# Seven key and value units of the memory between the stick-breaking heads

## What is computed

```python
# hgrn2 heads (4 of width 128) and stick-breaking heads (8 of width 64), side by side
z = jnp.einsum('bhtd,bhsd->bhts', q_blk, kh) * scale
log_beta = jax.nn.log_sigmoid(z)
log_one_minus = jnp.where(before, jax.nn.log_sigmoid(-z), 0.0)
between = lax.cumsum(log_one_minus, axis=3, reverse=True) - log_one_minus
weights = jnp.exp(jnp.where(before, log_beta + between, -jnp.inf))
o_sb = head_rmsnorm(weights @ v, sb_gnorm)
x = x + jnp.concatenate([o_hg, o_sb]) @ w_out
# cross-attention to a memory of 256 tokens, 4 heads of width 256
q = rmsnorm(x, mem_q_norm) @ w_q
k, v = jnp.split(rmsnorm(mem, mem_kv_norm) @ w_kv, 2)
x = x + (softmax(q @ k.T * 256 ** -0.5) @ v) @ w_o
```

## Time and profile before

| | us |
|---|---|
| median of 3 runs (lowest, highest) | 2531.74 (2530.05, 2534.24) |
| the profiled execution | 2530.41 |
| its span, first to last instruction | 2528.6 |
| PE busy in the span | 2443.9 (97%) |
| last step of Hgrn to the first values of Stick | 1821.9 to 1851.2 |
| values of head 0 to values of head 6 | 1851.2 to 1912.9 |
| values of head 6 to the end of the first unit of mix_out | 1912.9 to 1949.8 |
| key and value units | 1985.9 to 2028.0 |

### The profile page before, as it was taken

The page is one execution under the profiler, slowest core; times in us unless marked ns, Lnnn a source line. Parts: engine busy times, 40 slices in busy tenths (PEclk is TensorE's granted clock), DMA queues, the critical chain, the costliest instruction groups (busy, mean ns, idle before and its releaser), DMA issues.

```text
span 2528.6 us, 30307 instructions
## 1 busy us (share of the span) xinstructions
PE 2443.9 (97%) x12278; PEld 2034.2 (80%) x12278; DVE 1246.6 (49%) x1493; ACT 896.1 (35%) x1207; POOL 70.6 (3%) x80
## 2 busy tenths in 40 slices
PE   7989999999999999999999999999888999999998
PEld 6657888888899788888788888799866987888886
DVE  6687533357736543332444431546585645444423
ACT  3353333313344343331333321344444444333311
POOL 0210000000012000000000000000000000000000
PEclk9999999998999999999999999999988999999999
DMA  8125522363323122222222222221100322222221
GB/s 347 59 86 215 194 104 100 150 258 125 104 96 97 67 83 100 100 100 100 79 94 93 100 100 100 94 86 67 68 17 17 119 98 73 93 100 91 91 101 66
DMA packets 40408, 267.36 MB, mean 106 GB/s; under 512 B 4379, under 2 KB 5659, under 8 KB 9219
## 3 DMA queue, kind: packets, MB, share of 16 engines
q1 hardware_dynamic: 31248, 219.87, 24.2%
q0 software_dynamic: 5696, 40.37, 4.2%
q10 hardware_dynamic: 3378, 5.91, 0.8%
HBM read 263.90 MB, written 2.24 MB: 105 GB/s over the span
## 4 chain that ended last, share of the span: by engine, by line
PE 87%; DVE 7%; ACT 4%; issue 1%; DMA 0%; DVEq 0%; SPq 0%; ACTq 0%
PE bank L225 25%; PE bank L226 25%; PE bank L227 25%; DVE w_lo L212 1%; ACT w_hi L208 1%; PE bank L2107 1%; PE bank L328 1%; PE bank L2190 1%; PE bank L2202 1%; PE bank L1827 1%; DVE work L452 1%; PE bank L256 1%; DVE work L436 1%; PE bank L257 1%; PE bank L262 1%
## 5 line engine op out<-in xcount | busy, mean ns | idle before, releaser
L225 PE MATMUL bank<-h_hi,w_hi 128*128 128x512 f32 x1832 | 724.2, 395 | 5.4 <-DVE w_lo L212 2.2
L226 PE MATMUL bank<-h_lo,w_hi 128*128 128x512 f32 x1832 | 716.4, 391 | 0.0
L227 PE MATMUL bank<-h_hi,w_lo 128*128 128x512 f32 x1832 | 716.4, 391 | 0.0
L212 DVE TENSOR_TENSOR w_lo<-raw,w_hi 128x2048 fp32r<-128x2048 f32 x192 | 440.0, 2291 | 501.9 <-ACT w_hi L208 501.9
L208 ACT ACTIVATE w_hi<-raw 128x2048 fp32r<-128x2048 f32 x192 | 366.3, 1908 | 430.8 <-PE bank L227 425.6
L225 PEld LDWEIGHTS bank<-h_hi,w_hi 128*128 128x128 f32 x1832 | 346.0, 189 | 84.0 <-issue 6.7
L227 PEld LDWEIGHTS bank<-h_hi,w_lo 128*128 128x128 f32 x1832 | 345.8, 189 | 73.1
L226 PEld LDWEIGHTS bank<-h_lo,w_hi 128*128 128x128 f32 x1832 | 346.0, 189 | 71.8 <-issue 1.4
L227 PE MATMUL bank<-g_hi,w_lo 128*128 (+1 forms) x704 | 273.9, 389 | 0.0
L225 PE MATMUL bank<-g_hi,w_hi 128*128 (+1 forms) x704 | 273.9, 389 | 0.0
L226 PE MATMUL bank<-g_lo,w_hi 128*128 (+1 forms) x704 | 273.9, 389 | 0.0
(11 more groups left out here) (298 smaller groups left out, 2760.7 us busy)
## 6 DMA issues: line engine op xcount, KB each, us to landing
raw<-stream SPq DMA_DIRECT2D x192, 1024.0 KB, 4.8
work<-stream POOLq DMA_DIRECT2D x19, 1024.0 KB, 7.0
h_plain<-stream POOLq DMA_DIRECT2D x16, 1024.0 KB, 5.4
work<-stream SPq DMA_DIRECT2D x13, 1024.0 KB, 12.3
work<-mlstm_rows ACTq DMA_DIRECT2D x8, 512.0 KB, 5.0
x<-xT SPq DMA_DIRECT2D x1, 2048.0 KB, 9.6
outT<-work SPq DMA_DIRECT2D x8, 256.0 KB, 2.2
work<-mlstm_rows ACTq DMA_DIRECT2D x8, 192.0 KB
```

What stands on the lines that cost most here:

```text
L212: nc.vector.tensor_tensor(w_lo[:, slot(m), :], raw[:, slot(m), :], w_hi[:, slot(m), :], ALU.subtract).then_inc(lo_split, 1)
L225: nc.tensor.matmul(out, stationary[0], moving[0], start=first, stop=False)
L226: nc.tensor.matmul(out, stationary[0], moving[1], start=False, stop=False)
L227: return nc.tensor.matmul(out, stationary[1], moving[0], start=False, stop=last)
```

## The change

- `PLAN`: seven units `mem_kv` stand ahead of mix_out, and mem has five left (four of queries, one of values). Each of the seven is cut into four pieces of 12 matmuls, and the pieces are put into turns 2 to 8 of the loop over the heads.
- The memory is loaded and normed earlier, its three large multiplications on POOL (`Memory.gpsimd`), its root as exp(-0.5 ln). The masks of L2230 go from DVE to POOL.
- On DVE the part of head i-1 (L2226) now stands behind the part of head i. Unit splits stand between them on ACT and DVE.
- Roots of the Hgrn rows and of the first 6 stick heads are taken by logarithm and exponential (`LogTail`), inside the loop; mix_out reads mixed_hi and mixed_lo.
- The query norm isn't multiplied into the queries: `QueryNorm` gives one factor per token, used as scale of the exponentials of the attention; spreading it over rows (L487) falls away. The query projection gets x times the gain only.

```diff
@@ Stick.tensor, new
+                for i in range(self.H + 2):
+                    u = i - 2
+                    if i < self.H:
+                        self.score(pe, i)
+                    if i == 0:
+                        hg.sum_values(pe, hg.H - 1)
+                        pe.wait_ge(hg.s_out, hg.H)
+                        mem.sum_squares(pe)
+                        continue
+                    if 0 <= u < 7:
+                        mem.piece(pe, u, 0)
+                    if u >= 0:
+                        self.sum_values(pe, u)
+                    if i == self.H + 1:
+                        break
+                    if 0 <= u < 7 and i < self.H:
+                        mem.piece(pe, u, 1)
+                    for a in range(TB):
+                        self.sum_behind(pe, i - 1, a)
+                        if a == 1 and 0 <= u < 7:
+                            mem.piece(pe, u, 1 if i == self.H else 2)
+                    if i == self.H:
+                        for b in range(4):
+                            hg.tail.turn(pe, b)
+                        mem.piece(pe, u, 2)
+                    if 0 <= u < 7:
+                        mem.piece(pe, u, 3)
+                for b in range(3):
+                    pe.wait_ge(hg.tail.lo, b + 1)
+                    self.tail.turn(pe, b)
+                pe.wait_ge(self.s_x, TB * self.H)
+                self.next.first_chunks(pe, 0, 4)
+                self.tail.turn(pe, 3)
+                self.next.first_chunks(pe, 4, 6)
@@ Stick.vector
-                    h = i - 1
-                    if h >= 0:
-                        z = self.z[h % 2]
-                        for a in range(TB):
-                            n = TB * h + a
-                            dve.wait_ge(self.s_suf, n + 1)
-                            nc.vector.scalar_tensor_tensor(z[:, self.seg(a)], bank[:, 4 + n % 2, a * P:S], -1.0,
-                                                           z[:, self.seg(a)], ALU.mult, ALU.add).then_inc(self.s_x, 1)
...
+                    if 3 <= i < self.H:
+                        split_next_lo(dve, mem.m_kv + i - 3)
...
+                    h = i - 1
+                    if 0 <= h < self.H:
+                        for a in range(TB):
+                            n = TB * h + a
+                            dve.wait_ge(self.s_suf, n + 1)
+                            z = self.z[h % 2][:, self.seg(a)]
+                            nc.vector.scalar_tensor_tensor(z, bank[:, 4 + n % 2, a * P:S], -1.0, z, ALU.mult,
+                                                           ALU.add).then_inc(self.s_x, 1)
+                    if i == 0:
+                        for b in range(3):
+                            hg.tail.gate_rows(dve, b)
+                    if i == 1:
+                        hg.tail.gate_rows(dve, 3)
+                        split_next_lo(dve, mem.m_kv - 1)
+                        mem.low(dve)
@@ Stick.scalar
+                    if 3 <= i <= self.H:
+                        mem.evacuate(act, i - 3)
+                        split_next_hi(act, mem.m_kv + i - 3)
@@ Stick.gpsimd, new
+                for h in range(self.H):
+                    pool.wait_ge(self.s_x, TB * h + TB)
+                    z = self.z[h % 2]
+                    for a in range(TB):
+                        ins = nc.gpsimd.tensor_tensor(z[:, self.diag(a)], z[:, self.diag(a)], table("neg_strict"),
+                                                      ALU.add)
+                    ins.then_inc(self.s_nx, 1)
@@ Memory, new
+            def gpsimd(self, pool):
+                pool.wait_ge(mem_loaded, 16)
+                nc.gpsimd.tensor_tensor(self.sq, self.mt, self.mt, ALU.mult).then_inc(self.s_sq, 1)
...
+                pool.wait_ge(self.s_root, 1)
+                nc.gpsimd.tensor_tensor(t, t, self.rstd.unsqueeze(1).to_broadcast([P, KC, N_MEM]),
+                                        ALU.mult).then_inc(self.s_scaled, 1)
+            def piece(self, pe, u, j):
+                if j == 0:
+                    pe.wait_ge(lo_split, self.m_kv + u + 1)
+                    pe.wait_ge(self.s_lo, 1)
+                    if u:
+                        pe.wait_ge(self.s_kv, u)
+                last = self.kv_piece(self.m_kv + u, bank[:, 7, :].rearrange("p (a n) -> p a n", a=2), j, u < 4)
+                if j == 3:
+                    last.then_inc(unit_used, 1)
@@ Memory.exponents
-                                     bias=self.nm[:, s:s + 1], scale=256 ** -0.5,
+                                     bias=self.nm[:, s:s + 1], scale=self.norm.scores_by[:, t:t + 1],
```

More of the change, by code:

```diff
@@ L994, in wait_chunk, with take_roots, wait_roots, high @@
                         self.turn(pe, b + 2)
+        class LogTail(ToFeatures):
+            def take_roots(self, act, st, g0, g1):
+                act.wait_ge(self.sq, g1)
+                sums, logs, inv = (v.rearrange("p (t g) -> p t g", t=TB)[:, :, g0:g1]
+                                   for v in (self.sums, self.roots, self.inv))
+                st.link(nc.scalar.activation(logs, sums, ACT.Ln, bias=eps, scale=1.0 / self.group))
+                nc.scalar.activation(inv, logs, ACT.Exp, scale=-0.5).then_inc(self.root, 1)
+            def wait_roots(self, dve, n):
+                dve.wait_ge(self.root, n)
+            def high(self, act, b):
+                act.wait_ge(self.turned, b + 1)
+                nc.scalar.activation(mixed_hi[:, self.first + b, :], bank[:, b, :], ACT.Identity, bias=0.0,
+                                     scale=self.gain(b)).then_inc(self.hi, 1)
+            def low(self, dve, b):
+                dve.wait_ge(self.hi, b + 1)
+                nc.vector.scalar_tensor_tensor(mixed_lo[:, self.first + b, :], bank[:, b, :], self.gain(b),
+                                               mixed_hi[:, self.first + b, :], ALU.mult,
+                                               ALU.subtract).then_inc(self.lo, 1)
+            def turn(self, pe, b):
+                pe.wait_ge(self.rows_ready, self.per_chunk * (b + 1))
+                for t in range(TB):
+                    last = nc.tensor.transpose(bank[:, b, t * P:t * P + P], self.rows[:, t, b * P:b * P + P], ident)
+                last.then_inc(self.turned, 1)
         class Even:
@@ new lines, in sum_behind @@
+            def sum_behind(self, pe, h, a):
+                n = TB * h + a
+                if a == 0:
+                    pe.wait_ge(self.s_l, h + 1)
+                if n >= 2:
+                    pe.wait_ge(self.s_x, n - 1)
+                for j in range(a, TB):
+                    last = nc.tensor.matmul(bank[:, 4 + n % 2, j * P:S], table("tri") if j == a else ones,
+                                            self.l[h % 2][:, self.seg(j)], start=(j == a), stop=(j == TB - 1))
+                last.then_inc(self.s_suf, 1)
@@ L2305, in tensor, with __init__, take_inverse @@
                 self.sb.tensor(pe)
-                self.hg.tail.tensor(pe)
+        class QueryNorm(Norm):
+            deferred, spreads = True, False
+            def __init__(self, scale, before):
+                super().__init__(scale, None, 4, before)
+                self.sq = area(18432, KC, S)
+                self.scores_by = small[:, 488:488 + TB]
+            gain, low = Deferred.gain, Deferred.low
+            def take_inverse(self, dve, st):
+                dve.wait_ge(root_done, self.n + 1)
+                nc.vector.reciprocal(self.inv, self.root).then_inc(inv_done, 1)
+                dve.wait_ge(inv_done, self.n + 1)
+                st.link(nc.vector.tensor_scalar(self.scores_by, self.inv, 256 ** -0.5, None, ALU.mult))
         class Memory:
@@ new lines, in sum_squares, with root_and_high @@
+            def sum_squares(self, pe):
+                pe.wait_ge(self.s_sq, 1)
+                for k in range(KC):
+                    last = nc.tensor.matmul(bank[:, 7, 0:N_MEM], ones, self.sq[:, k * N_MEM:k * N_MEM + N_MEM],
+                                            start=(k == 0), stop=(k == KC - 1))
+                last.then_inc(self.s_ms, 1)
+            def root_and_high(self, act, st):
+                act.wait_ge(self.s_ms, 1)
+                st.link(nc.scalar.activation(self.logs, bank[:, 7, 0:N_MEM], ACT.Ln, bias=eps, scale=1.0 / D))
+                nc.scalar.activation(self.rstd, self.logs, ACT.Exp, scale=-0.5).then_inc(self.s_root, 1)
+                act.wait_ge(self.s_scaled, 2)
+                nc.scalar.activation(mem_hi.rearrange("p a n -> p (a n)"), self.t, ACT.Copy).then_inc(self.s_hi, 1)
@@ new lines, in low, with kv_piece @@
+            def low(self, dve):
+                dve.wait_ge(self.s_hi, 1)
+                nc.vector.tensor_tensor(mem_lo.rearrange("p a n -> p (a n)"), self.t,
+                                        mem_hi.rearrange("p a n -> p (a n)"), ALU.subtract).then_inc(self.s_lo, 1)
+            def kv_piece(self, m, out, j, keys):
+                wh, wl = unit_cols(m)
+                r = slice((j // 2) * P, (j // 2) * P + P)
```

(15 more changed lines are left out.)

354 lines of the change are left out of this document (151 added, 203 removed).

## The result

The changed kernel takes 2539.16 us (median of 16 runs, 2536.66 to 2547.61), the kernel before 2531.7 (16 runs beside them). The ratio is 1.0034, 95% interval 1.0024 to 1.0044: slower by 0.34%. The prediction's range, 2525 to 2543, holds it; its likeliest case (2534, no change that can be told) does not. The profiled execution took 2545.0 us, 5.8 more than the median, and is read here with that in mind; a second one is among the experiments.

The account below looks back on a forecast made before the run. PE, busy 97%, was taken to bound the kernel, a chain the Stick stretch. Start +2.9, loop +47.1, end -9.1, work taken away -44.6 and clock +6.0 gave +2.3 on 2530.4; as median 2534 us, range 2525 to 2543.

Parts of the forecast that it names:

- the start: Last Hgrn step to values of head 0: PE idles 7.1 us, POOL's 6.4 us product delays the memory; +2.9 us.
- the step 11.48 to key block 2: First half of a head's turn, from values to key block 2 on PE: 11.48 us, with PE idle 2.8.
- The taken-away 44.6: Seven units and the memory's sums of squares leave stretches where PE had no gap: 44.6 us gained in full.
- the end's -9.1: Values of head 6 to the end of mix_out's first unit: 27.8 us instead of 36.9, so -9.1.
- The first query unit: After mix_out: its input needs 2.4 us of the 4.1 available, so no delay, 1.7 us to spare.
- wait of 0.5 us for ACT's L2336: Second half of each head's turn: PE idles 0.5 us of 6.66 us, waiting for ACT.
- the clock in the loop: Gaps of 2.8 us bring the clock down in four of six heads, 1.5 us each: +6.0, bounds 0 to +20.
- -3.7: Sum of start, loop, end and work taken away, without the clock: -3.7 us.
- Rival C: Loop: more or longer clock falls, six of 2.0 to 2.5 us each, giving 2537 to 2543 us; chance 0.17.
- The loop's +47.1: Values of head 0 to values of head 6: six turns of 18.1 us, 108.8 instead of 61.7, so +47.1.
- the rival in which pieces fill the gaps: Loop: pieces fill PE's gaps as meant, a turn is PE's own 14.9 us, total 2508 us; chance 0.05.
- Rival B: Loop: POOL's masks become the chain if one takes over 0.97 us; 2549 us at 1.60 each; chance 0.09.

Follow-up runs that it names:

- e3: The changed kernel with five matmuls, whose result nobody reads, ahead of each head's third sum: 2538.9 us.
- f5: The kernel before with only two DVE blocks exchanged: log(1+e) and masks of a head ahead of the sums behind the previous head: 2594.85 us.
- e1: The changed kernel with DVE's work for the head before (L2297) put ahead of the new head's logarithm: 2518.2 us.
- f2: e1 with the four masks of each head moved from POOL back to DVE: 2515.79 us.
- f3: f2 with the memory's root one head earlier on ACT, its high part ahead of head 1's exponentials, its low part ahead of head 1's logarithm: 2508.01 us.
- f1: e1 and e5 together: the changed kernel with DVE's order corrected and the seven units behind the heads: 2563.33 us.
- e5: The changed kernel with the seven key and value units again behind the last head, everything else as changed: 2593.98 us.
- e2: The changed kernel with the memory's third large product on DVE, behind head 0's sums, instead of POOL: 2545.55 us.
- g1: f3 with both scalings of the memory on DVE, as eight instructions of 128x256, instead of POOL: 2509.75 us.
- g4: f5 with eight matmuls, whose result nobody reads, ahead of each head's third sum: 2576.77 us.

## Why the prediction was right or wrong

**Right.** The mechanism in a head: PE idle ahead of key block 2 because L2297 stands behind the new head's exp, ln, sum and masks (2.8 predicted, 2.67 measured), in five of six heads and once longer at the start (7.1 predicted, 9.4 measured); a head of 18.1 us, 17.76 at full clock, and the step 11.48 to key block 2 measured 1888.75 - 1877.53 = 11.22. The taken-away 44.6 and the end's -9.1 (-7.6; 1.5 of it a wait for ACT's L2336 at the last values) close the balance to 0.3 us. The first query unit was not delayed. One sign did not come: the wait of 0.5 us for ACT's L2336 in each head is absent, and key block 2 to the next values takes 6.54 us (6.66 predicted).

**Mis-sized: the start.** +2.9 predicted, +9.2 measured. The term took POOL's product at 6.4 us as a delay for the memory alone; it took 4.9, but it also held DVE's masks 4.2 us, and the product before it held |z| 2.3. That is 6.5, where 6.3 are missing, and the closeness is in part luck: the chain that the term added up (root, product, high part, low part) did not end last. The low part stood ready to start when the high part was done, but DVE reached it only behind the held masks, the sums, a gate and a unit split of 2.5 us; and the first piece ran at the low clock. The Trainium skill, SBUF — State Buffer, section "SBUF: two separate sides", states that the ports that VectorE and GpSimd share are locked for a whole instruction, by a GpSimd one or by a VectorE one with two SBUF inputs (this one against GpSimd work that reads SBUF), and that the other waits. The trace agrees (3.77 against 1.49, 3.70 against 2.28, and nothing on reads of PSUM). The prediction weighed how long GpSimd's product takes and never what it does to DVE.

**Mis-sized: the clock in the loop.** 6.0 predicted, bounds 0 to 20; 15.2 in one execution and 4.5 in the other. The prediction said four falls at 1.5 us each. The first execution had four in the loop, and they cost 13.2 us: 4.3 and 5.9 for the two that lasted 10.2 and 13.7 us, 1.1 to 1.9 for the two of 3.4. The second had two of 3.4 us, 1.0 and 1.5; the rest of both sums is the first head, which began at the low clock. So the count was right in one execution, and the size of 1.5 held for short falls alone. That the median lies nearer the smaller sum is inferred from e3.

**So the median.** -3.7 became +2.6 by the start alone (-3.7 + 6.3), and 1.5 of the end makes +4.1; six heads shorter by 0.34 take 2.0 off; with a clock term of 4.5 that is +6.6, against +7.5 measured. By this sum the side on which it ended, slower, was decided by the hold at the start, which no term had. The sum takes the part ahead of the end of Hgrn as unchanged, though it was 2.8 us shorter and 4.5 longer than before in the two executions, so a difference of 0.9 proves nothing. Rival C's 2537 to 2543 has the measured number, but its condition, six falls of 2.0 to 2.5 us, came in neither execution: the number is luck there.

**Wrong: what the parts are worth.** The loop's +47.1 was put down to units that have to be paid between heads, and the rival in which pieces fill the gaps (2508, 0.05) was given up because "the order of DVE's list" leaves no room. That the order leaves no room was right for this kernel; but the order is itself part of the change, and it was never priced by itself. f5 prices it in the kernel before: +64. e1 takes it back in the changed kernel: -21. With it corrected, the masks back on DVE (f2) and the memory's norm earlier (f3), the time is 2508, what that rival said: a head is then 14.8 us at full clock, PE's own work. Putting the units between the heads takes off 45 us in DVE's good order (f1 2563, e1 2518) and 55 in the bad one (e5 2594, 2539). Neither is what the idea gains over the kernel before: f1 itself stands 32 us above it, so a part of the 45 is that the units cover what POOL's masks cost. Over the kernel before, e1 is 13 us faster and f3 23.

**Rival B** was right in its kind and wrong in its place: in the changed kernel POOL's masks, 524 ns on average in the loop, are hidden. Once DVE's order is corrected they meet DVE's own masks and stand on the chain, 3.04 us for four beside units (e1, 0.35 us a head) and 3.13 without (f1).

What stays open: why e2's median is 6 us above the changed kernel, what the units win with the masks on DVE, why the part ahead of Hgrn's end differs by 7 us between executions, and whether the runs of g1 above 2509 are the clock or something else; their other executions left no trace.

## What to carry to other kernels

When a change fills one engine's idle time, look at whether it also reorders the engine that releases it, and price that order alone: here it cost 64 us by itself in the kernel before, and hid in the changed kernel a gain of 13 us (e1), or 23 with the masks and the norm moved too (f3). A gap on TensorE costs more than its length where the clock falls with it (in f5, gaps of 3.4 to 4.4 us: 18.9 us of idle time came with 33.7 of lower clock). Don't take the cost of such falls from one execution: here it was 15.2 us in one and 4.5 in the next. Before giving GpSimd a large product, list VectorE's instructions with two SBUF inputs that will meet it; put it beside copies out of PSUM, or off that engine.

## What the runs showed of the hardware that was not expected

- A DVE instruction with two inputs in SBUF that meets a running POOL product ends late by the rest of that product (2.28 to 3.70, 1.49 to 3.77 us, a mask of 0.29 to 4.47 within the 5.07), and POOL's short masks wait in the same way for DVE's long instructions (8.22 us for four). DVE's reads of a PSUM bank go on unchanged beside it.
- Where both engines have a row of such short instructions they alternate, 0.50 and 0.54 us each (f1, e1).
- The granted clock fell from 2.4 to 1.2 GHz in or behind gaps of 2.67 us in some heads and not in others of the same execution, and behind 1.95 us in g4; in the kernel before, gaps of 0.5 us had left it at 1.00 over six heads.
- POOL's products of 128x2048 took 3.60 us with a plain second input or a gain. The one with the root repeated along an axis took 4.92 in the changed kernel, where DVE's sum with two inputs in SBUF was still running over its first 0.57 us, and 5.36 in f2, where it ran over the first 1.01:

```profile
1845.94 5.36 POOL L2467 TENSOR_TENSOR h_plain<-h_plain 128x2048 f32<-128x2048 f32 x1 [14.90 <-ACT h_plain L2480]
```

So the product waited for DVE as well, and by that difference its own time is an estimated 4.35 us. Whether the form of the operand makes the rest, 0.75, was not tried.
